# A hybrid decoder block: tokens in natural order with earlier norms, in place of tokens kept residue by residue (mod 16)

## The reference

```python
u = rms_norm(h, mix_pre_g)
proj = u @ w_in                                    # 1024 -> 5120 columns
u_glu = proj[..., :2 * C_CONV]
p = proj[..., 2 * C_CONV:2 * C_CONV + C_POOL]
g_conv, g_pool = jnp.split(jax.nn.sigmoid(proj[..., 2 * C_CONV + C_POOL:]), 2, axis=-1)
# conv branch: a * sigmoid(gate), depthwise causal conv of width 31, layer norm, swish, @ w_conv_out
y_conv = conformer_conv_branch(u_glu, dw_kernel, dw_bias, conv_ln_g, conv_ln_b, w_conv_out)
# pooling branch: trailing mean over 2, 4, 8 or 16 tokens (by channel group) minus the token,
# a 256x256 linear per group, a scale per channel, @ w_pool_out
y_pool = pooling_branch(p, pool_w, pool_scale, w_pool_out)
h = h + rms_norm((g_conv * y_conv + g_pool * y_pool) @ w_o, mix_post_g)
v = jnp.square(jax.nn.relu(rms_norm(h, mlp_pre_g) @ w_ff1)) @ w_ff2
h = h + rms_norm(v, mlp_post_g)
```

## Time and profile before

| | us |
|---|---|
| median of 3 runs | 986.69 (985.55 to 987.22) |
| the profiled execution, slowest core | 985.55 |
| its span from first to last instruction (core 2; the cores: 981.7 to 984.0) | 984.0 |
| PE busy | 945.8 (96%) |
| DVE / ACT / POOL busy | 464.2 / 286.3 / 62.8 |
| mean granted TensorE clock of the cores, share of 2.4 GHz | 0.988 to 0.992 |

### The profile page before, as it was taken

The page is one execution under the profiler, slowest core; times in us unless marked ns, Lnnn a source line. Parts: engine busy times, 40 slices in busy tenths (PEclk is TensorE's granted clock), DMA queues, the critical chain, the costliest instruction groups (busy, mean ns, idle before and its releaser), DMA issues.

```text
span 984.0 us, 13888 instructions; the slowest of 8 cores (981.7 to 984.0 us)
## 1 busy us (share of the span) xinstructions
PE 945.8 (96%) x4843; PEld 455.7 (46%) x4843; DVE 464.2 (47%) x767; ACT 286.3 (29%) x531; POOL 62.8 (6%) x112
## 2 busy tenths in 40 slices
PE   7889959999999999999999999999999999999996
PEld 4654425545554444444444444444444444444444
DVE  4448998566556113466667640244223431233222
ACT  4674110123111721233334540233211330123211
POOL 1010000100001000121213200000000000000000
PEclk9999988999999999999999999999999999999998
DMA  9995043897687611759798997220022001210021
GB/s 176 256 148 69 4 69 44 134 130 119 105 122 123 124 49 63 113 135 178 175 178 175 208 194 112 79 93 1 1 86 78 8 2 43 86 43 1 1 86 65
DMA packets 109750, 95.39 MB, mean 97 GB/s; under 512 B 60241, under 2 KB 91217, under 8 KB 109554
## 3 DMA queue, kind: packets, MB, share of 16 engines
q0 software_dynamic: 32416, 35.13, 26.1%
q1 hardware_dynamic: 77266, 59.38, 23.6%
HBM read 98.88 MB, written 16.84 MB: 118 GB/s over the span
## 4 chain that ended last, share of the span: by engine, by line
PE 82%; DVE 7%; DMA 7%; issue 2%; ACT 1%; DVEq 0%; SPq 0%; POOL 0%; ACTq 0%; POOLq 0%
PE ps L222 82%; DMA arena<-w_pool_out 3%; DVE arena L243 2%; DMA arena<-w_in 2%; DVE arena L252 2%; DMA arena<-xh 1%; ACT arena L240 1%; DVE arena L248 1%; DVE arena L482 1%; DMA arena<-arena 1%; PE ps L225 0%; ACT sm L240 0%; SPq L265 0%; DVE arena L663 0%; POOL arena L268 0%
## 5 line engine op out<-in xcount | busy, mean ns | idle before, releaser
L222 PE MATMUL ps<-arena 128*128 128x512 bf16 (+4 forms) x4731 | 940.2, 361 | 25.4 <-DVE arena L248 10.4
L222 PEld LDWEIGHTS ps<-arena 128*128 128x128 bf16 (+1 forms) x4731 | 449.1, 99 | 511.7 <-issue 40.0
L240 ACT ACTIVATE arena<-ps 128x512 bf16<-128x512 f32 (+5 forms) x354 | 215.8, 619 | 624.1 <-PE ps L222 438.5
L248 DVE TENSOR_SCALAR ps<-ps 128x512 f32<-128x512 f32 x128 | 89.1, 699 | 111.2 <-PE ps L222 110.6
L243 DVE TENSOR_TENSOR ps<-ps,arena 128x512 f32<-128x512 f32 (+1 forms) x65 | 43.6, 688 | 176.3 <-ACT arena L240 175.8
L252 DVE SCALAR_TENSOR_TENSOR arena<-arena,ps 128x512 bf16<-128x512 f32 (+1 forms) x64 | 43.9, 686 | 123.8 <-ACT arena L240 123.8
L243 DVE TENSOR_TENSOR arena<-ps,arena 128x512 bf16<-128x512 f32 (+2 forms) x52 | 42.5, 830 | 31.0 <-ACT arena L240 25.9
L243 DVE TENSOR_TENSOR arena<-arena 128x512 bf16<-128x512 f32 (+2 forms) x56 | 41.3, 741 | 17.9 <-ACT arena L240 13.3
L240 ACT ACTIVATE arena<-arena 128x1024 bf16<-128x1024 f32 (+1 forms) x33 | 34.8, 1056 | 45.8 <-DVE arena L252 35.8
L252 DVE SCALAR_TENSOR_TENSOR arena<-ps,sm,arena 128x512 f32<-128x512 f32 (+1 forms) x65 | 45.1, 737 | 5.4 <-DVE sm L403 2.8
L252 DVE SCALAR_TENSOR_TENSOR arena<-arena,sm 128x1024 bf16<-128x1024 f32 (+1 forms) x33 | 42.3, 1282 | 4.1 <-POOL sm L399 2.1
(11 more groups left out here) (34 smaller groups left out, 91.7 us busy)
## 6 DMA issues: line engine op xcount, KB each, us to landing
arena<-xh SPq DMA_DIRECT2D x32, 512.0 KB, 8.9
arena<-w_ff POOLq DMA_DIRECT2D x16, 1024.0 KB, 28.0
out<-arena SPq DMA_DIRECT2D x31, 512.0 KB, 3.1
arena<-out SPq DMA_DIRECT2D x16, 512.0 KB, 4.3
arena<-w_in POOLq DMA_DIRECT2D x12, 512.0 KB, 14.0
arena<-w_in POOLq DMA_DIRECT2D x2, 2048.0 KB, 18.3
arena<-gb SPq DMA_DIRECT2D x4, 512.0 KB, 7.4
arena<-w_pool_out POOLq DMA_DIRECT2D x2, 1024.0 KB, 25.4
```

The lines of the kernel that those rows point to most:

```text
L222: kb.op("pe", lambda e: e.matmul(o, lhsT=l, rhs=r, start=start, stop=stop), [l, r], [o])
L240: kb.op("act", lambda e: e.activation(out=o, in_=i, func=func, **kw), rd, wr)
L248: kb.op("dve", lambda e: e.tensor_scalar(out=o, in0=a, scalar1=s1, scalar2=s2, op0=op0, **kw), rd, [o])
```

## The change

Tokens are kept in natural order from load to store. The weights of `glu_pair` become 128 columns of `uT` at a step of 16, `silu` reads its input with a step of 128 elements, and the views of step 16 in `pool_task` and `p_group` go. Pool tasks of the first two token blocks are queued before `pg`'s loop, and one task is taken out behind every `pg` and every `glu_pair`. The squares of `x_norm` go to two buffers `junk`; for tiles 8, 10, 12 and 14 GpSimd multiplies the tile by `gb0` and DVE only scales it. `nrm`s stand earlier in the list of `do`. `weff_scale` is split into four calls, made during `q = 2`.

```diff
     def x_load(j):
-            P, src = (32, xh[0:32, :]) if j < 0 else (128, xrows[j])
-            xev[j] = LOAD(xst[x_buf[x_order.index(j)]][:P], src.rearrange("p (k t) -> p k t", k=8),
+            P, r0 = (32, 0) if j < 0 else (128, H + 128 * j)
+            xev[j] = LOAD(xst[x_buf[x_order.index(j)]][:P], xh[r0:r0 + P, :].rearrange("p (k t) -> p k t", k=8),
...
+        junk = [av(RW + 2 * SLOT + i * 1024, 1024) for i in range(2)]
+        xgs = [c8(av(RW + 2 * SLOT + 2048 + i * 2048, 1024, dt=F32)) for i in range(2)]
...
-            r = rstd(src, P, 0, dst, "act")
-            STT(dst, src, r, c8(gb0)[:P], ALU.mult, ALU.mult)
+            if j in (8, 10, 12, 14):
+                xg = xgs[j // 2 % 2]
+                TTE("pool", xg, src, c8(gb0), ALU.mult)
+                TS(dst, xg, rstd(src, P, 0, c8(junk[i % 2]), "act"), ALU.mult)
+            else:
+                STT(dst, src, rstd(src, P, 0, c8(junk[i % 2])[:P], "act"), c8(gb0)[:P], ALU.mult, ALU.mult)
...
-            zo, z0 = zr[:, :, 32 * blk:32 * (blk + 1)], zr[:, :, 0]
-            tm = lambda v: v.rearrange("p (m r) -> p r m", r=16)
+            zo = z[:, cc, blk * 512:(blk + 1) * 512]
...
-            STT(zo, tm(sl), 1.0 / w, tm(pc[:, c0:c0 + 512]), ALU.mult, ALU.subtract)
+            STT(zo, sl, 1.0 / w, pc[:, c0:c0 + 512], ALU.mult, ALU.subtract)
...
-            COPY(eng, p_t[:, cc, 32:2080].rearrange("p (m r) -> p r m", r=16)[:, r0:r1, :],
-                 ps[:, b, h:n].rearrange("p (r m) -> p r m", m=128))
+            COPY(eng, p_t[:, cc, 32 + t0:32 + t0 + n], ps[:, b, 0:n])
...
-            (nrm, 5), (pu, 6, 1), (pu, 6, 0), (pu, 7, 1), (trn, 4), (pu, 7, 0), (trn, 5), (nrm, 6),
+            (nrm, 5), (pu, 6, 1), (pu, 6, 0), (pu, 7, 1), (trn, 4), (nrm, 6), (pu, 7, 0), (trn, 5),
...
+        for blk in range(2):
+            for cc in range(8):
+                pq(cc, blk)
         for blk in range(2, 4):
-            for cc in pools:
+            for cc in range(8):
                 pg(cc, blk)
-                if blk == 3:
-                    for b in range(4):
-                        pq(cc, b)
-                    pool_pump(1)
+                pq(cc, blk)
+                pool_pump(1)
...
-                    MM(ps[:, b + i, :], uT[:, k, H + r * 128:H + (r + 1) * 128], wg[q % 2][:, k, :, :].rearrange("p a n -> p (a n)"), k == 0, k == 7)
+                    MM(ps[:, b + i, :], uT[:, k, H + r:H + NT:16], wg[q % 2][:, k, :, :].rearrange("p a n -> p (a n)"), k == 0, k == 7)
...
-                pool_pump(2 if q == 0 else 1)
-                pump(3)
+                pool_pump(1)
+                if q == 2 and rp % 2 == 1:
+                    weff_scale(rp // 2)
+                pump(2)
...
-            ACT(s_t[:, cc, :].rearrange("p (r m) -> p r m", r=16), s_r[cc % 2], AF.Silu, bias=vcol(8, cc), scale=vcol(0, cc))
+            ACT(s_t[:, cc, :].rearrange("p (m r) -> p m r", r=16), s_r[cc % 2].rearrange("p r m -> p m r"), AF.Silu, bias=vcol(8, cc), scale=vcol(0, cc))
```

More of the change, by code:

```diff
@@ L189, in build_program @@
     out = nc.dram_tensor("out", [NT, DM], F32, kind="ExternalOutput").ap()
-    xrows = xh[H:TT, :].rearrange("(m r) d -> r m d", r=16)
-    orows = out.rearrange("(m r) d -> r m d", r=16)
     hud = nc.dram_tensor("hu_scratch", [H, DM], BF16, kind="Internal").ap()
@@ L468, in pool_task @@
                     TTE("dve", t1, t1, inv[:, 0, :], ALU.mult)
-                    STT(z0, pc[:, 32:48], -2.0, t1, ALU.mult, ALU.add)
+                    STT(zo[:, 0:16], pc[:, 32:48], -2.0, t1, ALU.mult, ALU.add)
                 return
@@ L490, in pool_task @@
                 TTE("dve", t1, sl[:, 0:16], inv[:, g, :], ALU.mult)
-                TTE("dve", z0, t1, pc[:, 32:48], ALU.subtract)
+                TTE("dve", zo[:, 0:16], t1, pc[:, 32:48], ALU.subtract)
         scr = T("scr", [128, 16 + 8], F32)
@@ L539, in build_program @@
             (pu, 0, 0), (pu, 1, 0), (pu, 2, 0), (pu, 3, 0), (pu, 4, 1), (pu, 4, 0), (nrm, 4), (pu, 5, 1), (pu, 5, 0),
[L540 to L544 removed]
+            (nrm, 5), (pu, 6, 1), (pu, 6, 0), (pu, 7, 1), (trn, 4), (nrm, 6), (pu, 7, 0), (trn, 5),
+            (pu, 0, 2), (nrm, 7), (pu, 1, 2), (trn, 6), (pu, 2, 2), (nrm, 8), (pu, 3, 2), (pu, 4, 2), (trn, 7), (nrm, 9), (pu, 5, 2),
+            (pu, 6, 2), (nrm, 10), (pu, 7, 2), (pu, 0, 3), (nrm, 11), (pu, 1, 3), (nrm, 12), (pu, 2, 3), (pu, 3, 3), (nrm, 13),
+            (pu, 4, 3), (pu, 5, 3), (nrm, 14), (pu, 6, 3), (nrm, 15), (pu, 7, 3), (wg_load, 0), (wg_load, 1)])
+        for blk in range(2):
+            for cc in range(8):
+                pq(cc, blk)
         for blk in range(2, 4):
[L546 removed]
+            for cc in range(8):
                 pg(cc, blk)
[L548 to L551 removed]
+                pq(cc, blk)
+                pool_pump(1)
         def conv_load(cc):
@@ L644, in weff_prep, with weff_scale @@
                 WLOAD(wpo[hh], wpo_v[:, :, hh * 512:(hh + 1) * 512], after=[cev[1]])
-        def weff_scale():
-            for g in range(4):
+        def weff_scale(g):
                 for jc in range(2):
@@ L681, in build_program @@
             if q == 2:
-                weff_scale()
                 WLOAD(wgp, w_in_v[:, :, 4096:5120], after=[cev[2]])
@@ L764, in x_reload @@
         def x_reload(j):
-            LOAD(xr[j % 3], xrows[j])
+            LOAD(xr[j % 3], xh[H + 128 * j:H + 128 * (j + 1), :])
         def resid_sq(p, c0, gb_t, junk, ac):
@@ L791, in resid_b @@
                         STT(rs, p, r, rs, ALU.mult, ALU.add)
-                rs, dst = res[:, c0:c0 + n], orows[j][:, c0:c0 + n]
+                rs, dst = res[:, c0:c0 + n], out[128 * j:128 * (j + 1), c0:c0 + n]
                 outh[j, c0] = kb.op("sp", lambda e, rs=rs, dst=dst: e.dma_start(out=dst, in_=rs), [rs], [("outh", j)], dma=True)
@@ L877, in ff2_end @@
             res = xres[j % 2]
-            LOAD(res, orows[j], reads=[("outh", j)])
+            LOAD(res, out[128 * j:128 * (j + 1), :], reads=[("outh", j)])
             resid_b(halves(b), resid_a(b, gb3, 0, hT[j // 4][:, 0, :], "act"), res, j)
```

7 lines of the change are left out of this document (1 added, 6 removed).

## The result

The changed kernel takes 975.65 us (median of 4 runs, lowest 973.32) beside 986.17 (median of 4, 985.55 to 987.22): ratio 0.9884, 95% interval 0.9863 to 0.9905, some 11 us less. The forecast was 969.3 in a range of 958 to 1001. Executions in which some cores ran at a lower clock than the rest (one of the changed kernel at 995.71, half of e5's) are left out of all ratios.

A forecast was written before the change was run, and what follows sets the result against it. PE's 0.213 us matmul pitch was the floor, with losses at the start's join and to DVE in q = 0 and q = 1. 985.55 - 4.7 - 18.8 + 6.7 + 0.5 = 969.25, so 969.3 us, range 958 to 1001.

The forecast's parts named there:

- Norms, -4.7: Start: earlier squares let the third token block begin at 54.0 instead of 58.66 us; bounds 0 to -6.5.
- The walk: Start: count of ACT's queue from tile 4's square to tile 11's, 44.3 us without waits, 47.3 taken.
- a rival for q = 1: DVE still lags, through GpSimd or longer edge work; half of the 19.5 us stays, 979.0 us; chance 0.08.
- The statement that loads may stay as they are: Start: loads go in the same order into the same buffers, so their landings were left unchanged.
- the norms are not earlier: Rival: ACT's queue stops at a copy waiting for PE, third block starts near 58, 974.0 us; chance 0.05.
- Pool tasks, -18.8: q = 0 and q = 1: earlier, shorter pool tasks end DVE's lag, -19.5 + 0.7 us; bounds -10 to -19.5.
- the +0.7: q = 1: part added back to the -19.5 us, with DVE's work at 35.5 us against 34.93.
- Scaling, +6.7: q = 2: weff_scale waits for poolwT, a PE stop of 4.9 us plus 1.8 at half clock; bounds 0 to 9.
- The rival without it: q = 2: poolwT is not late, so the 6.7 us fall away, 962.6 us; chance 0.07.
- Strided weights, 0: GLU blocks: 512 strided weight loads take 0.19 us each, hidden under matmuls of 0.213 us, no cost.
- the rival that held most of the other side: GLU blocks: strided weight loads come out from under the matmul, deciding from 245 ns; 250 ns or more, chance 0.26.
- silu, +0.5: GLU: strided read lengthens a silu from 2.09 to 3.5 us, costing 0.5 us; bounds 0 to 3.

The follow-up runs named there:

- e5: Changed kernel with pool tasks queued as in the kernel before, operands still contiguous; lowest 984.03 us, ratio 1.001 to the kernel before.
- e1: Changed kernel with all norm products on DVE, none on GpSimd; 975.07 us, ratio 0.9870 to the kernel before.
- e2: Changed kernel with contiguous weight loads in the GLU, which then works on other tokens; 976.14 us, ratio 0.9887 to the kernel before.
- e3: Changed kernel with the four weff_scale calls back behind the block of q = 2; 970.86 us, ratio 0.9832 to the kernel before.
- e4: Changed kernel with all norm products on DVE and weff_scale behind q = 2; 968.11 us, ratio 0.9804 to the kernel before.
- e8: Changed kernel with the norms, start list and buffers of the kernel before; 973.33 us, ratio 0.9868 to the kernel before.
- e9: Changed kernel with the old norms, list and buffers, and weff_scale behind q = 2; 968.9 us, ratio 0.9816 to the kernel before.
- e11: e4 run again beside e9; 968.01 us, ratio 0.9803 to the kernel before.
- e6: e1 with only the first eighth of the columns of tiles 13 to 15 loaded, the rest stale; 972.86 us, ratio 0.9858 to the kernel before.

## Why the prediction was right, and which step failed

The direction and the largest term held. The distance to the profiled execution is 975.57 - 969.25 = 6.3 us, and the terms put it in one place: start +2.7 for -4.7 (7.4 off), q = 0 and q = 1 -17.8 for -18.8 (1.0), scaling +6.3 for +6.7 (-0.4), silu and the rest -1.2 for +0.5 (-1.7). The range held because the two largest terms, q = 0 and q = 1 and the scaling, came as forecast.

*Norms, -4.7: the step that failed.* The third block was to start at 54.0 and starts at 58.72. The step led from tile 11's square by ACT's queue, a product of the old duration and a landing 3.5 us on; of these 4.7 us, the square has 2.2, the root and inversion 0.5 (2.5 us for 2.0), the product 1.8 and the landing 0.1.

First, ACT reached the square at 49.52 instead of 47.3. The walk gave 3.0 us for all of ACT's waits; on core 3, where tile 4's square even began 1.6 us earlier, ACT stands 5.9 us for PE at two copies, each right in front of a square (tiles 7 and 10):

```profile
39.21 0.38 ACT L238 ACTIVATE arena<-ps 128x256 f32<-128x256 f32 x1 [3.36 <-PE ps L220]
47.49 0.38 ACT L238 ACTIVATE arena<-ps 128x256 f32<-128x256 f32 x1 [2.54 <-PE ps L220]
...
45.04 0.61 PE L223 MATMUL ps<-identb,arena 128*128 128x128 bf16 x8 [1.99 <-ACT sm L238]
```

PE was late for the second of them because it stood for the transposes of tile 7 (third line; it names ACT, but the product that they read ended later, at 44.79), and this product took 3.40 us beside GpSimd's. In e1, without GpSimd, this second wait is 0.42 us on core 1, while the first is 3.36 there too; the square begins at 49.16. (The row taken for a contiguous copy in the earlier trace rows is the halo's sigmoid, 32 partitions; the copies of 256 columns measured 0.378, so nothing hangs on it.)

Second, the product of tile 11 took 3.08 us on DVE. The rows of the start show how: GpSimd's product runs from 51.65 to 54.01 and DVE's ends 1.08 later, at 55.09; the one from 46.79 ends at 49.15, DVE's at 50.24, 1.09 later. A DVE product that begins second thus gets hardly further than if it began at the other's end. Whoever begins first is not held up: on core 7, DVE's product of tile 7 began first and kept its time, and GpSimd's ended 2.22 behind it (44.89 for 42.67).

```profile
41.38 1.29 DVE L250 SCALAR_TENSOR_TENSOR arena<-arena,sm 128x1024 bf16<-128x1024 f32 x1
42.23 2.66 POOL L241 TENSOR_TENSOR arena<-arena 128x1024 f32<-128x1024 f32 x1 [1.36 <-DMA arena<-xh]
```

The Trainium skill (Trainium Architecture — The Big Picture, What this means for kernel authors) says that DVE and GpSimd lock each other out of a port they share, and do not split it; this trace agrees for a DVE operation with two operands of 1,024 f32. The prediction had this only as half a sentence of a rival for q = 1 ("get in each other's way"); the price lay here. Kernels with GpSimd products reach the halo of q = 0 at 87.7 to 88.6 us on the mean (changed, e2, e3, e5), those without at 85.5 to 86.6 (e1, e4, e8, e9, e11; the table's first two columns added): about 2 us for four products that were to save DVE time.

Third, an earlier product helps only if its transpose is issued and lands. In the changed kernel this does not show: tile 11's is issued 0.14 us after its product and lands 3.3 later. But it would have stopped the step even so: e1 ended tile 11's product at 52.65, and its transpose was issued 1.7 us later, behind transposes that took up to 7.9 us; e6 took bytes off the DMA and brought the block 2.1 us forward. The statement that loads may stay as they are held for the loads; it forgot that the transposes stand behind them.

The stretch at the lower clock that follows was not in the sum. It is no new effect: from the third block to the halo of q = 0 six cores of before already took 29.0 to 29.4 us, cores 2 and 4 27.7, and core 2 was the profiled one; the means are 28.9 and 29.0. So 2.6 of the start's 7.4 us (30.35 on core 3 for 27.72) come from setting two different cores side by side. Nor did DVE's lag hide it before. DVE stood for the results of the fourth block before it could begin the pool tasks (core 2):

```profile
75.71 1.05 DVE L243 TENSOR_TENSOR arena<-arena 128x512 bf16<-128x512 f32 x1 [13.35 <-ACT arena L240]
```

So what delays PE there delays DVE too: from the third block to the third sigmoid the six cores took 114.7 us on the mean, the two 113.1 (single cores scatter by 1.8). In e6, after stops of 1.2 to 2.1 us, no core shows the stretch; after 3.27 to 4.14, in the changed kernel, six of eight do.

The cores now differ by 8 us for two reasons in the table's rows: they reach the halo of q = 0 within 3.0 us of each other (86.1 to 89.1), and the q = 2 block adds 36.3 to 41.2; without the latter (e3) they differ by 5.

The time lies nearest the rival *the norms are not earlier* (974.0), and its observation was right. Its reason, a copy in front of a square, is the first of the three.

*Pool tasks, -18.8.* Measured -17.8 on the slowest core, -17.3 on the mean. PE kept its pitch; what remains is waits like the 1.2 us above, where q = 1 was forecast without reserve. e5 shows the order to be the larger share, as the step said. (By its own numbers, 35.5 for 34.93, the +0.7 in it would be 0.6.)

*Scaling, +6.7.* Measured +6.3, with the stop where it was put, DVE idle for `poolwT` ahead of it and half clock behind it; e3 removes all of it. Only the split is other than 4.9 and 1.8: the stop is 3.42, as `poolwT` took 7.2 us on core 3 and not 8.7, and the rest of the block's 6.3, the half clock above all, is 2.8. That the sum agrees is in part luck. The rival without it happens in part on cores 0, 2 and 5, but the slowest core sets the time.

*Strided weights, 0.* The estimate of 0.19 to 0.22 us was too high, 0.145 was measured, 47 ns more than contiguous, and e2 shows that nothing of it reaches the end. So the rival that held most of the other side fails by 100 ns. The Trainium skill's rule of 16-byte lines (SBUF — State Buffer, Door 1: The DMA port swizzle) agrees in kind. The Trainium skill (TensorE: Matmul & The Clock Gate, Weight-path perf modes) gives the column steps that the fast weight load allows, and no price for them; what the prediction read into it, a load as fast as a contiguous one, is not so here (0.145 for 0.098). A sum by either comes out the same.

*silu, +0.5.* Its duration was right (3.91, between 3.5 and 3.95); it cost nothing: what follows q = 2 is the same within 0.1 us on the mean.

What stays open: what makes PE late for the copy in front of tile 7's square, which waits 3.36 us with GpSimd and without, and why `poolwT` lands faster on some cores, before and after.

## What to carry to other kernels

Before work is moved to GpSimd, look which DVE operations will run beside it, and which begins first: four products cost some 2 us where they were to save time. A chain is as early as its last queue, so follow it through the DMA queue too, behind loads that nobody waits for yet; and a load that is moved out of its way must not end up between its links. Compare the same stretch on all cores before a difference is put down to the change: the stretch at half clock behind the third block was in six of the eight cores before, and not in the profiled one. And work moved ahead of a critical operation must have its data by then: the scaling in q = 2, which waited for `poolwT`, cost a third of the gain until it went back to its place.

## What the runs showed of the hardware

- A DVE product with two operands of 128x1024 f32 takes 1.28 us alone. Where GpSimd's product of the same shape (2.36) began first, it ended 1.08 or 1.09 after that one, and took 1.46 to 3.40 by when it began (all cores of the changed kernel); where it began first, it kept its time and GpSimd's ended about 2.2 after it.
- A bf16 weight load of 128x128 with a step of 32 bytes takes 0.145 us, a contiguous one 0.097 or 0.098; under a matmul of 512 columns (0.213) the difference is hidden.
- An ACT operation of 2,048 bf16 columns takes 3.91 us when read with a step of 256 bytes, 2.09 contiguous.
- A DMA transpose of 128x1024 bf16 lands 3.1 us after its issue when the loads of `x` are through, and 7.9 behind them (e1, core 1).
